# Exchanging the rotary halves of an attention projection: products by a permutation on TensorE replaced by a round trip through device memory

## What is computed

```python
def apply_rope(x, cos, sin):
    xf = x.astype(jnp.float32)
    half = xf.shape[-1] // 2
    x1, x2 = xf[..., :half], xf[..., half:]
    return jnp.concatenate([x1 * cos - x2 * sin, x2 * cos + x1 * sin], axis=-1).astype(x.dtype)
...
    for l in range(DEPTH):
        h = rms_norm(x, pre_norm[l])
        proj = h @ w_in[l]
        (dq, dk, dv, dgate, gq, gk, gv, ggate, mq, mgate) = jnp.split(proj, IN_OFFSETS, axis=-1)
        dq = apply_rope(dq.reshape(...), *lin_cs)          # groups of 32 channels: halves of 16
        dk = apply_rope(dk.reshape(...), *lin_cs)
        gq = apply_axial_rope(rms_norm(gq, gqa_q_norm[l]), row_cs, col_cs)
        gk = apply_axial_rope(rms_norm(gk, gqa_k_norm[l]), row_cs, col_cs)
        ...
```

## Time and profile before

| | |
|---|---|
| median of 3 runs | 2801.74 us (2801.63 to 2803.39) |
| the profiled execution's own time | 2802.95 us |
| its span | 2801.1 us |
| TensorE busy | 2699.8 us, 96% of the span |
| VectorE, ScalarE, POOL busy | 51%, 39%, 25% |
| mean DMA rate over the span | 96 GB/s |

### The profile page before, as it was taken

How to read it: one execution, slowest core, us unless ns; L and a number is a source line. 1 busy time by engine, 2 the same in 40 slices (tenths; PEclk the granted TensorE clock), 3 DMA queues, 4 the chain that set the end, 5 groups by cost and what they waited for, 6 DMA issues and landing times.

```text
span 2801.1 us, 35940 instructions
## 1 busy us (share of the span) xinstructions
PE 2699.8 (96%) x13734; PEld 2219.0 (79%) x13734; DVE 1442.6 (51%) x1988; ACT 1099.5 (39%) x1787; POOL 697.3 (25%) x601
## 2 busy tenths in 40 slices
PE   6998999999999999999999999999999998999998
PEld 6875688766788888888798888887888886988887
DVE  5566655664475442587364442465432774644423
ACT  3357643376443422423352222342222475422222
POOL 1037430165368700245020000156000200200000
PEclk9999999999999999999999999999999999999999
DMA  3320023200144423444222323345223443232232
GB/s 128 120 76 1 16 69 117 73 31 1 46 92 134 145 77 97 134 136 143 96 76 91 103 76 93 102 165 217 90 83 99 157 149 99 76 101 93 76 94 71
DMA packets 307740, 269.26 MB, mean 96 GB/s; under 512 B 44595, under 2 KB 297948, under 8 KB 304028
## 3 DMA queue, kind: packets, MB, share of 16 engines
q1 hardware_dynamic: 300780, 241.71, 27.9%
q0 software_dynamic: 2800, 20.25, 1.8%
q10 hardware_dynamic: 4032, 5.57, 0.7%
HBM read 239.74 MB, written 27.77 MB: 95 GB/s over the span
## 4 chain that ended last, share of the span: by engine, by line
PE 75%; DVE 7%; POOL 5%; issue 3%; ACT 3%; POOLq 2%; DVEq 2%; SPq 1%; DMA 1%; ACTq 0%
PE bank L421 22%; PE bank L422 22%; PE bank L423 22%; POOL E L1830 2%; POOLq L1829 2%; PE bank L1992 2%; PE bank L1318 2%; DVE XL L481 1%; ACT WH L383 1%; POOL MBB L796 1%; POOL MBA L796 1%; DVE X L585 1%; DVE work L581 1%; DVE WL L388 1%; PE bank L1978 1%
## 5 line engine op out<-in xcount | busy, mean ns | idle before, releaser
L421 PE MATMUL bank<-XH,WH 128*128 128x512 f32 (+1 forms) x2400 | 901.5, 376 | 36.2 <-DVE WL L388 13.6
L422 PE MATMUL bank<-XL,WH 128*128 128x512 f32 (+1 forms) x2400 | 890.9, 371 | 0.0
L423 PE MATMUL bank<-XH,WL 128*128 128x512 f32 (+1 forms) x2400 | 889.3, 371 | 0.0
L388 DVE TENSOR_TENSOR WL<-raw,WH 128x2048 fp32r<-128x2048 f32 (+1 forms) x208 | 443.6, 2133 | 537.2 <-ACT WH L383 536.9
L421 PEld LDWEIGHTS bank<-XH,WH 128*128 128x128 f32 x2400 | 456.1, 190 | 133.5 <-DVE WL L388 18.9
L383 ACT ACTIVATE WH<-raw 128x2048 fp32r<-128x2048 f32 (+1 forms) x208 | 362.5, 1743 | 460.2 <-PE bank L423 459.7
L422 PEld LDWEIGHTS bank<-XL,WH 128*128 128x128 f32 x2400 | 456.8, 190 | 84.6 <-issue 3.3
L423 PEld LDWEIGHTS bank<-XH,WL 128*128 128x128 f32 x2400 | 456.2, 190 | 81.8
L1115 POOL TENSOR_TENSOR ssq<-ssq,sq 128x512 f32<-128x512 f32 x24 | 30.9, 1289 | 1075.3 <-ACT sq L1024 1075.3
L422 PE MATMUL bank<-HL,WH 128*128 128x512 f32 (+1 forms) x792 | 293.9, 371 | 0.0
L423 PE MATMUL bank<-HH,WL 128*128 128x512 f32 (+1 forms) x792 | 293.4, 370 | 0.0
(11 more groups left out here) (410 smaller groups left out, 3643.3 us busy)
## 6 DMA issues: line engine op xcount, KB each, us to landing
raw<-in_ffn_w_dram SPq DMA_DIRECT2D x88, 1024.0 KB, 5.3
raw<-in_ffn_w_dram SPq DMA_DIRECT2D x64, 704.0 KB, 4.6
raw<-in_w_in_dram SPq DMA_DIRECT2D x24, 1024.0 KB, 5.2
MM<-mm_scr SPq DMA_DIRECT2D x12, 1152.0 KB, 7.4
raw<-in_w_out_dram SPq DMA_DIRECT2D x8, 1024.0 KB, 5.1
raw<-in_cv_w_in_dram SPq DMA_DIRECT2D x8, 1024.0 KB, 5.5
mm_scr<-MBA POOLq DMA_DIRECT2D x6, 1152.0 KB, 4.7
mm_scr<-MBB POOLq DMA_DIRECT2D x6, 1152.0 KB, 4.5
```

Source lines behind the costliest of these rows:

```text
L388: dve.tensor_tensor(WL[:, slot, 0:n * P], raw[:, slot, 0:n * P], WH[:, slot, 0:n * P].bitcast(F32), ALU.subtract).then_inc(l_done, 1)
L421: pe.matmul(out, WH[:, slot, c:c + P], h, start=start, stop=False)
L422: pe.matmul(out, WH[:, slot, c:c + P], l, start=False, stop=False)
L423: return pe.matmul(out, WL[:, slot, c:c + P], h, start=False, stop=stop)
```

## The change

Each of the ten blocks is written twice to a scratch tensor in device memory, into rows 0 to 31 and 32 to 63 of its group of 64 rows, and read back from row 16 on: the 32 rows that come back are the group with its halves exchanged. SyncE issues all of it: for the first six blocks the writes stand between the loads of b6 and b7 and the reads between b7 and b8; for the last four both stand between b12 and b13. The read-back blocks land in the two slots of work1 and in PR blocks 16, 17, 20 and 21, which are free at that time (`exchanged(n)`). `turn(n)` waits for all six, or for all ten. The products and their waits are gone from TensorE; banks 6 and 7 are no longer used for them.

```diff
+        swap_scr = nc.dram_tensor("swap_scr", [10, P // 32, 4, 16, T], F32).ap()
...
+        def exchanged(n):
+            j = (0, 1, 16, 17, 20, 21, 20, 21, 0, 1)[n]
+            return work1[:, j, :] if j < 2 else PR[:, j, :]
...
-            for n in range(4, 12):
+            def swap_out(n):
+                j = ROPED[n][0]
+                if j >= GQ:
+                    sp.wait_ge(ss(s, "gn"), at(s, "gn", j - GQ + 1))
+                else:
+                    sp.wait_ge(acc_read, tiles_before[s] + acc_of(j) + 1)
+                for i in range(2):
+                    sp.dma_start(swap_scr[n, :, 2 * i:2 * i + 2].rearrange("g o c t -> g (o c) t"), PR[:, j, :])\
+                      .then_inc(ss(s, "swap_out"), 16)
+            def swap_in(n):
+                sp.wait_ge(ss(s, "swap_out"), at(s, "swap_out", 32 * (6 if n < 6 else 10)))
+                if n >= 6:
+                    sp.wait_ge(ss(s, "roped"), at(s, "roped", 6))
+                sp.dma_start(exchanged(n), swap_scr[n, :, 1:3].rearrange("g o c t -> g (o c) t"))\
+                  .then_inc(ss(s, "swapped"), 16)
+            in_block(4)
+            for n in range(6):
+                swap_out(n)
+            in_block(5)
+            for n in range(6):
+                swap_in(n)
+            for n in range(6, 11):
                 in_block(n)
+            for n in range(6, 10):
+                swap_out(n)
+            for n in range(6, 10):
+                swap_in(n)
+            in_block(11)
             out_sp(sp, b0 + 14, io["w_out"][l])
...
-            def swap(n):
-                j = ROPED[n][0]
-                if j >= GQ:
-                    pe.wait_ge(ss(s, "gn"), at(s, "gn", j - GQ + 1))
-                if n >= 2:
-                    pe.wait_ge(ss(s, "roped"), at(s, "roped", n - 1))
-                pe.matmul(bank[6 + n % 2][:, :], perm[:, 0, :], PR[:, j, :], start=True, stop=True)\
-                  .then_inc(ss(s, "swapped"), 1)
...
-            swap(0)
-            swap(1)
             block(5)
-            swap(2)
-            swap(3)
...
-            block(8, lambda: (swap(6), swap(7)))
+            block(8)
             value_turn(3)
-            block(9, lambda: (swap(8), swap(9)))
+            block(9)
...
-                dve.wait_ge(ss(s, "swapped"), at(s, "swapped", n + 1))
+                dve.wait_ge(ss(s, "swapped"), at(s, "swapped", 16 * (6 if n < 6 else 10)))
                 dve.tensor_tensor(PR[:, j, :], PR[:, j, :], rope[:, tab, :], ALU.mult)
-                dve.tensor_tensor(work1[:, n % 2, :], bank[6 + n % 2][:, :], rope[:, tab + 1, :], ALU.mult)
+                dve.tensor_tensor(exchanged(n), exchanged(n), rope[:, tab + 1, :], ALU.mult)
                 dve.drain()
-                dve.tensor_tensor(PR[:, j, :], PR[:, j, :], work1[:, n % 2, :], ALU.add).then_inc(ss(s, "roped"), 1)
+                dve.tensor_tensor(PR[:, j, :], PR[:, j, :], exchanged(n), ALU.add).then_inc(ss(s, "roped"), 1)
```

More of the change, by code:

```diff
@@ L347, in program @@
             "attn": dict(mem_in=32, rope_in=16, mem_n=2, ml=KD, mem_t=KD, mh=KD, mrms=1, msq=2, vm_t=1, vmh=1, vml=1,
-                         v_t=4, vh=4, vl=4, gsq=4, gms=4, gln=4, grms=4, gn=4, swapped=10, roped=10, ready=1, gate=8,
+                         v_t=4, vh=4, vl=4, gsq=4, gms=4, gln=4, grms=4, gn=4, swap_out=16 * 20, swapped=16 * 10, roped=10, ready=1, gate=8,
                          s=91, e=91, nb=64, p=24, pn=40, rsum=64, scaled=24, qh=14, ql=14, pt=64, pt_a=52, pt_d=12, pv=32, o=16, osq=3, orms=3, og=3,
@@ L1911, in attn_pe @@
             block(6, lambda: head_squares(1))
-            swap(4)
-            swap(5)
             value_turn(1)
```

## The result

The changed kernel takes **2902.15 us** (median of 4 runs, 2896.94 to 2903.63) against 2801.68 us (4 runs, 2798.91 to 2803.39) for the kernel before: a ratio of 1.0357, 95% interval 1.0345 to 1.037. That is 100 us slower. The profiled execution of it took 2896.94 us, with a span of 2895.1 us, 94.0 us more than before.

A forecast was written before the change was run, and what follows sets the result against it. TensorE was taken as the bound, busy 96% of the span with 75% of the chain. A layer loses 38.0 - 1 + 1.5 = 38.5 us, 77 for both: 2802.95 plus 77 is 2880, 2879 against the median; range 2850 to 2920.

The forecast's parts named there:

- the forecast: Exchange transfers: four engines carry each, 2.2 to 3.0 us apiece, weight blocks queue behind; likeliest 2879 us, chance 0.77.
- Rival A: Exchange transfers: all sixteen engines carry each, 0.65 us an engine; 2795 us, chance 0.14.
- Rival B: SyncE's queue: four engines, but weight blocks do not queue behind the exchange; 2840 us, chance 0.05.
- Rival C: Exchange writes: four engines and writes much dearer, 3.5 us a transfer; 2939 us, chance 0.04.
- What is taken away: TensorE's twenty swaps: 17.0 us, and 4.8 us of waits for head norms; at most 21.8 us saved.
- The first batch: Twelve writes and six reads around b7: weights and head norms late, 14.3 us a layer.
- The walk: Step-by-step timeline of the first layer, doubled for the second; first exponential 38.0 us late.
- b7 and tables 118.5, six reads 15.6, b8 2.7: 136.7: First layer's DMA queue up to b8's transfer at 136.7 us; b8 landed at 138, ready at 142.2.
- The sum: A layer's total: 38.0 late, less 1, plus 1.5, is 38.5 us; 77 us for both layers.
- The second batch: Eight writes and four reads after the head norms: turn(6) at 209.2 instead of 163.85 us.
- The signs: Profile after: DMA share near 0.25, about 100 GB/s; TensorE waits some 10, 8, 24 us; twelfth write landing in 30 us.
- That costs nothing: SyncE's queue before b7: twelve writes at 0.37 us of issuing each, 4.4 us of otherwise idle queue.

The follow-up runs named there:

- E1: The change with 128 outer rows on the scratch side instead of 4 groups of 32, halves not exchanged; 2798.64 us.
- E2: The change with no exchange at all, neither products nor transfers; VectorE multiplies each block itself by the sine; 2780.72 us.
- E5: The change with the 1 MB load of the sine and cosine tables released one block of weights later; 2902.2 us.
- E9: The change with b9 issued only once VectorE has finished turn(0), so that b8 moves without it; 2913.27 us.
- E4: The change for blocks 0 to 5 only; blocks 6 to 9 exchanged by TensorE's products as before; 2840.61 us.
- E8: Against the change: sixteen-partition pieces straight from PR to the exchanged block, no device memory; b13 before the second batch, turn(6) awaiting its pair alone; 2790.30 us.
- E10: E8 with VectorE's evict(8) and low_w(12) moved ahead of turn(6) and turn(7); 2787.23 us.
- E11: The change with the scratch side in eight groups of sixteen rows instead of four of thirty-two, rows unexchanged; 2820.45 us.
- E7: The change with one 128-row write for two blocks and eight sixteen-row reads, full exchange through device memory; 2803.89 us.
- E6: The change with b13 loaded ahead of the second batch of writes instead of behind its reads; 2898.44 us.

## Why the prediction was right, and where its sizes were off

**The direction and the mechanism.** Of the cases, the forecast came: four engines for each transfer (a share of 0.26 at 102 GB/s), everything else in line behind them (ScalarE took b7 up at 122.18 us, before at 99.12). 2902.15 lies in the range, 23 us above the point. Rival A was excluded by the share of 0.26, and E1 shows its world: 2798.6 where I worked out 2795. In its world a measurement can't tell it from no change. Rival B needed b7 ahead of the writes; it was taken up at 122.18. Rival C had a price of 3.5 us a transfer; it is 2.57, inside my 2.5 to 2.6.

**What is taken away.** 17.0 and up to 4.8 us were the estimate; E2 measured 20 to 21. Right.

**The first batch.** The walk had b7 ready at 121; `low_w(7)` ended at 126.4, 4.7 us later by the clock that starts with b6. It had `block(6)` at 142.2, 63.2 us after b6's issue; it started at 147.03, 67.2 after. These 4.0 us are b8's landing, taken up 63.0 instead of 59.0 us after b6's issue. The step that failed is the sum "b7 and tables 118.5, six reads 15.6, b8 2.7: 136.7". Of the 4.0 us, 1.6 were there when b7 was taken up: 121.4 us by the walk's clock, where b7 and tables at 118.5 and a landing of 1.3 give 119.8. Twelve writes at 2.57 instead of 2.5 us are 0.8 of them. The other 2.4 us came with the reads and b8. Moving the tables' load within the busy stretch (E5) did not help, and b9 accounts for 0.6 us at most (E9). What stays open is the rest: from 132 to 134 us the share was 1.13 at only 226 GB/s, so that the engines were busy and moved little. With b9 held back (E9) the same window has 1.11 at 231 GB/s, so b9 isn't the cause of it either, and I have no run that says what is. That the wait before `block(6)` reads 4.6 us and names `Vm`, not `low_w(8)`, is the same lateness: the copy to `Vm` stands behind b8's rounding on ScalarE. From `block(6)` to the first head norm's end it took 32.8 us, 1.2 more than in the walk, about what the half clock took: it was granted at 0.50 from 146 to 148 us, and from the start of the block's first product to that of its fourth it took 2.1 us, where 1.1 was usual. The sum has 1.5 us for it, a term that no run shows: the runs show the 0.50 of these 2 us, as in the earlier trace rows, and the 1.0 us more that the block's first products took.

**The second batch.** From the first head norm's end (179.84) to the issue of the reads: 24.4 us, expected 22.5. From there to `turn(6)`: 14.5, expected 12.9. The transfers themselves fit (8 and 4 times 2.57 are 20.6 and 10.3). The failed term is the fixed part of a run of transfers, which I took as 2.5 us from the 1.95 of the earlier trace rows: it is 3.8 and 4.2, which is 3.0 us more for the two. The transfers' own size adds some 0.5, so about 3.6 us a layer were missing. From `turn(6)` to `ready` it took 18.5 us instead of 17.7; `low_w(13)` took 3.06 us there instead of 2.29.

**The sum.** 4.0 + 1.2 + 3.6 + 0.8 = 9.6 us a layer over the walk's 38.0: the 47.6 us measured. Over the sum's 38.5 that is 9.1 us, 18 for both layers; the other 5 of the 23 us above the point are the distance from the profiled execution to the median (2896.94 to 2902.15). The split was off too: E4 gives the first batch 19.5 us a layer, with its own swaps' savings counted, where I had 14.3.

**The signs.** Share and rate came as named, apart from the tables' load in the middle, and so did ScalarE's waits for b7 and b8 and VectorE's for the reads. TensorE's waits of 10, 8 and 24 us came as 15.0, 4.6 and 28.9, the first two under other names. One sign failed: the view by transfers gives no landing time for the writes, and 30 us for the twelfth did not come about. SyncE began to issue it only at about 105.6 us, 13.7 us before the reads could go out, because the issues that I had at 0.37 us each (4.4 us, "That costs nothing") held the queue for 28.06. That step was wrong too, and it cost nothing that I can see.

## What to carry to other kernels

Before a transfer replaces arithmetic, look at the outermost count of both its patterns. Here, with four groups of 32 rows, a quarter of the DMA engines carried a transfer (a share of 0.26 at 102 GB/s against 1.05 at 404 with 128 rows), so that 256 KB took 2.57 us instead of 0.65, and what stood behind it on the queue waited: b7 reached ScalarE 23 us later than before. In E8 and E10 the halves were exchanged in pieces of sixteen partitions straight within SBUF, 11 and 14 us faster than with the products, at a price of 5 to 6 us of issuing for two blocks. In E8 VectorE idled 5.8 and 4.4 us behind it; with other work in that pause E10 was 3.1 us faster still. And before holding a load back, list what stands behind its consumer's wait, not only when the product needs it (E9).

## What the runs showed of the hardware that I had not expected

- **Issuing was not cheap where four engines carried the transfers.** I counted 0.37 us for each of twelve issues; they held SyncE for 28.06 us (2.3 us a write, not much less than the 2.57 that one takes to move), against 12.15 in E11 (a share of 0.52) and 8.04 in E1 (about 1). After the first ones the queue took the next transfer about as fast as the earlier ones moved: from 90.47 us on, three took 7.57 us, 2.52 each. I take it to have cost nothing more here, since the share was 0.25 or more in every 2 us from 80 to 110 us and b7 would have waited on the engines anyway. Other work of that queue would have been held up, as b7's issue was until 108.31 us.
- **The issue's price differed with the two sides.** 64 KB pieces cost 0.45 us from device memory (E7: 8 in 3.56), 0.62 within SBUF (E8: 8 in 4.94), and up to 0.8 for the pair before `turn(6)` of the first layer (8 in 6.36, in E10 in 6.14). Why these were dearer is not shown; the same eight of E8 took 4.95 us in the second layer.
- **A wait's name is not its cost.** The longest wait of ScalarE (32.2 us for b13) was worth at most 2 us a layer (E6), and 0.4 by the traces.
